# Six norms of a four-layer block: products on rows that are not yet normalised

## The chip, the cores and the metric

The kernel runs as one program on one core of a Trainium2 chip. The metric is the device time of one execution, in microseconds. TensorE (PE) multiplies, VectorE (DVE), ScalarE (ACT) and GpSimd (POOL) work on tiles of 128 partitions, and SyncE (SP) issues the transfers.

## What is computed

The input x is 256 tokens of 1024 channels. Four layers follow one another, two of a first kind and two of a second; each has a mixing part and a feed-forward part, and each part begins with an RMS norm:

```python
# first kind: norms before and after each part
h = rmsnorm(x, norm_mix_pre[l]);  z = h @ w_in[l]
x = x + rmsnorm(merged @ w_o[l], norm_mix_post[l])
h = rmsnorm(x, norm_ffn_pre[l]);  up = causal_dwconv(h @ w_up[l], ffn_conv_w[l])
x = x + rmsnorm((silu(gate) * val) @ w_down[l], norm_ffn_post[l])
# second kind: norms only before each part
xn = _rms(x, norm_mix_g);  z = xn @ w_in
x = x + merged @ w_out
xn = _rms(x, norm_ffn_g);  x = x + (silu(xn @ w_g) * (xn @ w_u)) @ w_down
# the norm
rmsnorm(x, g) = x * rsqrt(mean(x * x) + eps) * g
```

The factor rsqrt(...) is one number for each token, so that (x * g * factor) @ w is the same as ((x * g) @ w) * factor.

## The kernel before

**Layout.** x lies channel-major in X: eight row tiles of 128 channels by 256 tokens. All weights come as one stream of 582 pieces of 128 x 1024 (512 KB), each with eight blocks of 128 x 128. A ring of five buffers takes each piece from memory (F); ACT rounds it to H (high part), DVE subtracts it into L (low part), and PE uses both. DVE makes the low part of a piece at most four pieces ahead of PE, since the ring has five buffers. A product of one weight block with one row tile is three matmuls of 256 columns: high by high (HH), high by the row's low part (HL), low by high.

**Norms.** There are eight, numbered b = 0 to 7: b = 2 * layer for the mixing part, one more for the feed-forward part. Norms 1 to 4 (SUMMED) sit on the output of a post-norm of the first kind: there the last product of the layer before gives Z, the sum of squares of Z gives a first factor ("s1"), X becomes X + Z * factor, and only then comes the second factor ("s2") of the new X. Norms 0, 5, 6 and 7 are plain: one factor. In each norm PE adds the squares over partitions with a matrix of ones, ACT takes a root, DVE takes the reciprocal and makes a diagonal (line 1143), PE spreads it over the partitions (s1 or s2), and DVE multiplies the eight rows (line 1234 plain, line 1199 summed). ACT rounds each row to HH (line 1922), DVE (even rows, line 1248) and POOL (odd rows, line 2445) make HL. PE issues some idle matmuls (keep_busy) meanwhile, and then the first products of the next part.

**Order.** Nothing is scheduled at run time: every engine has its own program in a fixed order, written by functions that walk over the same list of groups. A group is one output tile of 128 columns (24 matmuls) or, where four are woven, four tiles in four PSUM banks (96 matmuls); a token group ("t", the values v, m_v) has 512-column products in two banks. PE takes the four banks in turn, and waits before a group until the bank's last reader (ACT or DVE) is done. `settle(n)` reads the banks of group n and stands in the programs beside group n + 1. In the mixing part of the first kind the groups are: the woven cf_b0, cf_a0, cf_b1, cf_a1, then cf_b2, cf_a2, cf_b3, cf_a3, then q0, q1, k0, k1, v, g_ret and so on. DVE also runs the 31 taps of a long convolution there (lines 1466 and 1470), four instructions beside each group. In the second kind they are: the woven i_q0, i_q1, gate8, i_k, then the token group m_v, then m_q0, m_q1, m_q2. In the feed-forward part: the woven fg0, fv0, fg1, fv1, then fg2, fv2.

**Swaps.** q and k are turned by a rotation; SP copies them with partitions exchanged (line 2626), and DVE waits for it (line 1302). SP issues weight pieces in front of the swap, and piece j of the stream waits until the low part of piece j - 5 is made:

```python
def asked(n):
    return G[n].pos // PB + 9
...
pieces_to(asked(group_of(l, name, 1) + 1))
swap(name, l, member(l, name, 1))
```

If p0 is the first piece of the woven group, q0 is piece p8, k0 is p10, and the swap of q waits for the issue of p18, and so for the low part of p13.

## Time and profile before

| | |
|---|---|
| median of 3 runs | 1834.47 us (1834.27 to 1837.68) |
| profiled execution, first to last instruction (span) | 1830.6 us |
| runs' median less that span (start and end of the program) | 3.9 us |
| PE busy | 1777.5 us, 97% of the span |
| DVE busy | 1360.9 us, 74% |
| ACT busy | 1073.6 us, 59% |
| granted TensorE clock | full in all 40 slices |

The profile was taken in one execution; no time of its own is given for that execution beside its span. A sum of parts is made against the span, and the 3.9 us around it are taken as unchanged. Times in a trace are counted from the first instruction. A row of the trace gives the start, the duration, and in brackets how long the engine was idle before it and what it waited for.

### The profile page before, as it was taken

The numbers are of one execution on the slowest core, as the hardware profiler recorded it, in microseconds if no ns is written. First come the engines' busy times: TensorE is split into PE (matmuls) and PEld (weight loads), VectorE is DVE, ScalarE is ACT, GpSimd is POOL, SyncE is SP. The second block draws the span as 40 slices with busy tenths as digits, with TensorE's granted clock in tenths as the row PEclk, the third lists the DMA queues.
The fourth block names the chain that finished last, engine by engine and source line by source line (L and its number), as shares of the span: only waits on it lengthen the run. The fifth ranks groups of instructions, "written<-read, shape, count | busy, mean of one in ns | idle before, by whom it ended". The sixth has DMA issues, their size and how long they took to land.

```text
span 1830.6 us, 36315 instructions
## 1 busy us (share of the span) xinstructions
PE 1777.5 (97%) x14784; PEld 1731.1 (95%) x14784; DVE 1360.9 (74%) x2385; ACT 1073.6 (59%) x1808; POOL 191.1 (10%) x200
## 2 busy tenths in 40 slices
PE   8999999999999999999999989999999998999998
PEld 8999999999999999999999879999999998899998
DVE  6898789867889779876768868655557697686553
ACT  5455666655455657654776576544458757755442
POOL 1002410001002410001201003000002100020000
PEclk9999999999999999999999999999999999999999
DMA  7545546564645536664645634556545564346563
GB/s 282 175 158 185 182 138 201 194 207 143 204 160 180 184 128 209 194 206 140 193 150 169 203 104 143 180 196 196 194 151 184 161 200 130 107 168 197 196 195 105
DMA packets 90341, 320.06 MB, mean 175 GB/s; under 512 B 10528, under 2 KB 12992, under 8 KB 90048
## 3 DMA queue, kind: packets, MB, share of 16 engines
q1 hardware_dynamic: 90176, 317.75, 53.7%
q8 instruction: 117, 1.92, 0.4%
q14 instruction: 48, 0.39, 0.1%
HBM read 310.60 MB, written 1.08 MB: 170 GB/s over the span
## 4 chain that ended last, share of the span: by engine, by line
PE 74%; DVE 15%; ACT 5%; issue 3%; POOL 1%; DMA 1%; SPq 0%; DVEq 0%; ACTq 0%; POOLq 0%
PE big L589 68%; PE small L589 4%; DVE L L1113 4%; DVE POOL L1470 4%; ACT H L1889 1%; PE small L588 1%; DVE POOL L1302 1%; DVE POOL L1668 1%; POOL POOL L2485 1%; ACT POOL L2311 1%; ACT POOL L2273 1%; ACT L1985 0%; POOL POOL L2464 0%; DVE FL L1280 0%; DVE POOL L1309 0%
## 5 line engine op out<-in xcount | busy, mean ns | idle before, releaser
L589 PE MATMUL big<-HH,H 128*128 128x256 f32 x3344 | 940.1, 281 | 5.3 <-ACT HH L1922 3.3
L589 PE MATMUL big<-HL,H 128*128 128x256 f32 x3344 | 925.2, 277 | 3.9 <-DVE HL L1248 3.8
L589 PE MATMUL big<-HH,L 128*128 128x256 f32 x3344 | 924.3, 276 | 0.0
L1113 DVE TENSOR_TENSOR L<-F,H 128x1024 fp32r<-128x1024 f32 x574 | 703.8, 1235 | 203.0 <-ACT H L1889 201.7
L1889 ACT ACTIVATE H<-F 128x1024 fp32r<-128x1024 f32 x582 | 610.7, 1055 | 205.7 <-PE big L589 202.8
L589 PEld LDWEIGHTS big<-HH,H 128*128 128x128 f32 x3344 | 628.2, 188 | 10.7 <-issue 5.5
L589 PEld LDWEIGHTS big<-HL,H 128*128 128x128 f32 x3344 | 628.4, 188 | 7.5 <-DVE HL L1248 5.7
L589 PEld LDWEIGHTS big<-HH,L 128*128 128x128 f32 x3344 | 627.9, 188 | 0.0
L589 PE MATMUL big<-FH,H 128*128 128x256 f32 x848 | 238.5, 281 | 0.0
L589 PE MATMUL big<-FH,L 128*128 128x256 f32 x848 | 234.4, 276 | 0.0
L589 PE MATMUL big<-FL,H 128*128 128x256 f32 x848 | 234.4, 276 | 0.0
L589 PEld LDWEIGHTS big<-FH,H 128*128 128x128 f32 x848 | 159.3, 188 | 1.4 <-issue 1.0
L589 PEld LDWEIGHTS big<-FL,H 128*128 128x128 f32 x848 | 159.3, 188 | 1.1 <-issue 1.0
L589 PEld LDWEIGHTS big<-FH,L 128*128 128x128 f32 x848 | 159.2, 188 | 0.0
L1470 DVE SCALAR_TENSOR_TENSOR POOL<-POOL,PR 128x256 f32<-128x256 f32 x240 | 104.1, 498 | 0.1
L589 PE MATMUL small<-POOL 128*128 128x128 f32 (+2 forms) x352 | 79.8, 347 | 11.5 <-DVE FL L1712 7.3
L589 PE MATMUL big<-ffn,H 128*128 128x256 f32 x512 | 88.4, 276 | 0.0
L589 PEld LDWEIGHTS big<-ffn,H 128*128 128x128 f32 x512 | 77.1, 188 | 0.0
L589 PEld LDWEIGHTS small<-POOL 128*128 128x128 f32 x352 | 53.0, 189 | 19.4 <-DVE FL L1712 9.2
L589 PE MATMUL big<-ffn,L 128*128 128x256 f32 x256 | 70.7, 276 | 0.0
L1371 DVE SCALAR_TENSOR_TENSOR POOL<-big,PR,POOL 128x255 f32<-128x255 f32 x88 | 42.2, 479 | 22.1 <-ACT POOL L2067 17.7
L2440 POOL TENSOR_TENSOR X<-X,POOL 128x256 f32<-128x256 f32 x16 | 15.1, 945 | 407.5 <-DVE POOL L1216 407.5
(237 smaller groups left out, 1797.4 us busy)
## 6 DMA issues: line engine op xcount, KB each, us to landing
F<-in_stream SPq DMA_DIRECT2D x582, 512.0 KB, 4.0
POOL<-POOL SPq DMA_DIRECT2D x32, 128.0 KB, 3.9
POOL<-head_rows SPq DMA_DIRECT2D x8, 256.0 KB, 5.1
X<-in_x SPq DMA_DIRECT2D x2, 512.0 KB, 4.8
POOL<-POOL SPq DMA_DIRECT2D x16, 64.0 KB, 3.0
out_x<-X SPq DMA_DIRECT2D x1, 1024.0 KB, 3.9
POOL<-in_decay SPq DMA_DIRECT2D x1, 768.0 KB, 11.1
POOL<-POOL SPq DMA_DIRECT2D x8, 96.0 KB, 5.7
```

Source lines behind the costliest of these rows:

```text
L588: return pe.e.matmul(out_, lhsT, rhs, start=start, stop=stop, skip_group_check=True)
L589: return pe.e.matmul(out_, lhsT, rhs, start=start, stop=stop)
L1113: v.tensor_tensor(L[:, j % NR, :], F[:, j % NF, :], H[:, j % NR, :].bitcast(F32), ALU.subtract).then_inc(s_lo, 1)
L1302: v.tensor_tensor(rows, rows, factor, ALU.mult).then_inc(rp_v[name].sem, rp_v[name].up(l, part))
L1371: v.scalar_tensor_tensor(out=dst[:, 1:T], in0=ps[:, 0:T - 1], scalar=par("ffn_w", l, 44 + row), in1=dst[:, 1:T], op0=ALU.mult, op1=ALU.add ...
L1470: r = v.scalar_tensor_tensor(out=acc, in0=glu[:, j, k:k + T], scalar=par("cf_w", l, k * 4 + j), in1=acc, op0=ALU.mult, op1=ALU.add)
L1668: r = v.tensor_tensor_reduce(out=p[:, e * nk:(e + 1) * nk], in0=bank[:, e * nk:(e + 1) * nk], in1=mask, scale=1.0, scalar=LOW, op0=ALU.add ...
L1889: a.activation(H[:, j % NR, :], F[:, j % NF, :], ACT.Copy).then_inc(s_hi, 1)
L2273: r = a.activation(p[:, e * nk:(e + 1) * nk], p[:, e * nk:(e + 1) * nk], ACT.Exp, bias=mx[:, e:e + 1], scale=root_of_queries("s_q", qt, pa ...
L2311: r = a.activation(p[:, e * nk:(e + 1) * nk], p[:, e * nk:(e + 1) * nk], ACT.Exp, bias=mx[:, e:e + 1], scale=root_of_queries("d_q", qt, h) ...
L2440: q.tensor_tensor(X[:, n, :], X[:, n, :], tile(Z + n), ALU.add).then_inc(bnd_g.sem, bnd_g.up(b, "x", n))
L2485: q.tensor_tensor(tile(dst), tile(x), tile(y), ALU.add).then_inc(lc_g.sem, lc_g.up(l, event))
```

## The change

For six norms (RAW: 0, 2, 4, 5, 6, 7) the first groups are computed from rows x * g that don't carry the token factor. RAW gives how many groups: five after norms 0 and 2, two after 4 and 6, one after 5 and 7. ACT rounds x * g (high_raw), DVE makes its low part (low_raw), into memory that is free at that time (ROUND, ffn). PE begins with these rows, and forms the sums and the spreading matmuls between the products of the woven group (beside_row); at a summed norm only the second factor is put off, the first is still needed for X. ACT copies the spread factor to a tile S in SBUF. DVE then multiplies each raw result by S from PSUM to a tile RAWT (scaled_out), and the former readers read RAWT; the token group m_v gets the factor as a scale of ACT's copy. The normalised rows are still made (normal_rows, high_rows), for the groups after the raw ones: beside the raw groups, two rows at a time. The order of the woven group's 96 matmuls changes: for each row four high-by-high, four high-by-low, four low-by-high. At the start SP issues the gains of norm 0 and the first weight piece before x. The idle matmuls of the six norms go.

```diff
+RAW = {0: 5, 2: 5, 4: 2, 5: 1, 6: 2, 7: 1}
...
+            def raw_blocks(g):
+                b, n = g.raw, len(g.members)
+                banks_ = [bank_for(m)[:, 0:T] for m in g.members]
+                for k in range(KT):
+                    if k == 3:
+                        yield
+                    places = []
+                    for i in range(n):
+                        j, o = divmod(g.pos + k * n + i, PB)
+                        places.append((j, H[:, j % NR, o * P:(o + 1) * P], L[:, j % NR, o * P:(o + 1) * P]))
+                    m = g.members[0]
+                    xh, xl = x_of(m, k)
+                    wait_x(m, k, False)
+                    for ps, (j, hi, lo) in zip(banks_, places):
+                        pe.wait_ge(s_hi, j + 1)
+                        mm(ps, hi, xh, start=(k == 0), stop=False)
+                    wait_x(m, k, True)
+                    for ps, (j, hi, lo) in zip(banks_, places):
+                        mm(ps, hi, xl, start=False, stop=False)
+                    for i, (ps, (j, hi, lo)) in enumerate(zip(banks_, places)):
+                        pe.wait_ge(s_lo, j + 1)
+                        r = mm(ps, lo, xh, start=False, stop=(k == KT - 1))
+                        if k == KT - 1 or (k * n + i + g.pos) % PB == PB - 1:
+                            r.then_inc(s_mm, 1)
+                    beside_row(b, k)
+            def beside_row(b, k):
+                if b in SUMMED:
+                    if k == 6:
+                        pe.wait_ge(bnd_v.sem, bnd_v.at(b, "dg2"))
+                        mm(use(3, b, "s2")[:, 0:T], ones, tile(DG + 1)).then_inc(s_fill[3], 1)
+                    return
+                if k == (6 if b == 0 else 0):
+                    if b == 0:
+                        bank = use(0, b, "yy")
+                        pe.wait_ge(s_ones, 16)
+                        pe.wait_ge(bnd_v.sem, bnd_v.at(b, "add", 0, 7))
+                        wide_sums(bank, (0, 1), tile(YSQ), True, True).then_inc(s_fill[0], 1)
+                    else:
+                        sums_of(b, 7, False, True)
+                if k == (7 if b == 0 else 2):
+                    pe.wait_ge(bnd_v.sem, bnd_v.at(b, "dg"))
+                    mm(use(2, b, "s1")[:, 0:T], ones, tile(DG)).then_inc(s_fill[2], 1)
+            def raw_norm(b):
+                if b not in SUMMED:
+                    return
+                yy, zx = use(0, b, "yy"), use(1, b, "zx")
+                pe.wait_ge(bnd_v.sem, bnd_v.at(b, "add", last_added(b)))
+                wide_sums(yy, (0, 1), squares_at(0), True, False)
+                pe.wait_ge(bnd_a.sem, bnd_a.at(b, "sq", 7))
+                wide_sums(yy, (0, 1), squares_at(7), False, True).then_inc(s_fill[0], 1)
+                wide_sums(zx, (0, 2), squares_at(0, 1), True, False)
+                wide_sums(zx, (1, 3), squares_at(0, 2), False, False)
+                pe.wait_ge(bnd_v.sem, bnd_v.at(b, "dg"))
+                mm(use(2, b, "s1")[:, 0:T], ones, tile(DG)).then_inc(s_fill[2], 1)
+                pe.wait_ge(bnd_a.sem, bnd_a.at(b, "zz", 7))
+                wide_sums(zx, (0, 2), squares_at(7, 1), False, False)
+                pe.wait_ge(bnd_v.sem, bnd_v.at(b, "xz", 7))
+                wide_sums(zx, (1, 3), squares_at(7, 2), False, True).then_inc(s_fill[1], 1)
...
+            def low_raw(b, k):
+                gain, l = gain_of(b)
+                dve.wait_ge(rh_a.sem, rh_a.at(b, k))
+                v.scalar_tensor_tensor(out=raw_low(b, k), in0=X[:, k, :], scalar=par(gain, l, k),
+                                       in1=raw_high(b, k).bitcast(F32), op0=ALU.mult, op1=ALU.subtract).then_inc(
+                    rl_v.sem, rl_v.up(b, k))
...
+            def raw_norm(b):
+                first = begun_pieces(first_of(b))
...
+                if b in SUMMED:
+                    product_of_sums(b, 7)
+                was_read(b, "yy")
+                v.reciprocal(col(4, 2), col(2, 2)).then_inc(bnd_v.sem, bnd_v.up(b, "r"))
+                dve.wait_ge(bnd_v.sem, bnd_v.at(b, "r"))
+                diagonals(col(4, 2), tile(DG), bnd_v, b, "dg")
+                if b in SUMMED:
+                    raw_rows(b)
+                    return
+                if b:
+                    dve.wait_ge(s_evd, (last_of(b // 2, "out") if b % 2 else last_of(b // 2 - 1, "down")).dve)
+                    low_raw(b, 7)
+                    low_parts(first + AHEAD + 1)
+                if b % 2:
+                    for pair in range(4):
+                        normal_rows(b, pair)
+                        if pair == 2:
+                            low_parts(first + AHEAD + 2)
...
+            def raw_rows(b):
+                u = kept(b)
+                scaled(b, 0)
+                added(b, 0)
+                for n in range(KT):
+                    if n % 2 == 0:
+                        for i in (n + 1, n + 2):
+                            if i < KT:
+                                scaled(b, i)
+                    if n % 2:
+                        dve.wait_ge(bnd_g.sem, bnd_g.at(b, "x", n))
+                    else:
+                        dve.wait_ge(bnd_v.sem, bnd_v.at(b, "x", n))
+                    low_raw(b, n)
+                    if n % 2 == 0 and n + 2 < KT:
+                        added(b, n + 2)
...
+            def normal_rows(b, pair):
+                layer, e = use_of(b)
+                gain, l = gain_of(b)
+                was_read(b, "s2" if b in SUMMED else "s1")
+                dve.wait_ge(s_par, 16)
+                for n in (2 * pair, 2 * pair + 1):
+                    v.scalar_tensor_tensor(out=normal(b, n), in0=X[:, n, :], scalar=par(gain, l, n), in1=S,
+                                           op0=ALU.mult, op1=ALU.mult).then_inc(bnd_v.sem, bnd_v.up(b, "full", n))
+                low_x(b, 2 * pair)
+            def scaled_out(m):
+                b, i = m.raw
+                was_read(b, "s2" if b in SUMMED else "s1")
+                if i >= 4:
+                    before = [x for g in G if g.raw == b for x in g.members][i - 4]
+                    dve.wait_ge(s_eva, before.act)
+                    dve.wait_ge(s_evd, before.dve)
+                dve.wait_ge(s_mm, m.done)
+                v.tensor_tensor(landed(m), big[m.banks[0]][:, 0:T], S, ALU.mult).then_inc(
+                    raw_v.sem, raw_v.up(b, i))
...
             def settle(n, low=0):
-                for m in G[n].members:
-                    if low:
+                for i, m in enumerate(G[n].members):
+                    if m.raw and m.kind != "t":
+                        scaled_out(m)
+                    if low and (i % 2 == 0 or not m.raw):
                         low_parts(low)
...
+                pairs = pairs_in(n)
                 for j in first:
+                    if len(pairs) > 1:
+                        normal_rows(g.raw, pairs.pop(0))
                     low_parts(j + AHEAD)
                 if not made_after and not tapped and not full_banks(n - 1):
                     settle(n - 1)
+                for pair in pairs:
+                    normal_rows(g.raw, pair)
...
+            def high_raw(b, k):
+                gain, l = gain_of(b)
+                a.activation(raw_high(b, k), X[:, k, :], ACT.Copy, scale=par(gain, l, k)).then_inc(
+                    rh_a.sem, rh_a.up(b, k))
...
+                bank, read = is_filled(b, "yy")
+                root(col(2, 2), sums_in(bank), D).then_inc(read, 1)
+                if b in SUMMED:
+                    square_of_sums(b, 7)
+                    high_parts(first + AHEAD + 1)
+                    for n in range(KT):
+                        if n % 2:
+                            act.wait_ge(bnd_g.sem, bnd_g.at(b, "x", n))
+                        else:
+                            act.wait_ge(bnd_v.sem, bnd_v.at(b, "x", n))
+                        high_raw(b, n)
+                        if n in (3, 5):
+                            high_parts(first + AHEAD + n // 2 + 1)
+                    act.wait_ge(bnd_v.sem, bnd_v.at(b, "u"))
+                    root(col(6, 2), kept(b), D).then_inc(bnd_a.sem, bnd_a.up(b, "v"))
+                tables(layer, e)
+                if b not in SUMMED and b:
+                    high_parts(first + AHEAD + 2)
+                bank, read = is_filled(b, "s2" if b in SUMMED else "s1")
+                a.activation(S, bank[:, 0:T], ACT.Copy).then_inc(read, 1)
+                if b % 2:
+                    for pair in range(4):
+                        high_rows(b, pair)
+                        if pair % 2 == 0:
+                            high_parts(first + AHEAD + 3 + pair // 2)
+            def high_rows(b, pair):
+                layer, e = use_of(b)
+                for n in (2 * pair, 2 * pair + 1):
+                    act.wait_ge(bnd_v.sem, bnd_v.at(b, "full", n))
+                    a.activation(HH[:, n, :], normal(b, n), ACT.Copy).then_inc(hh.sem, hh.up(layer, e, n))
...
+                pairs = pairs_in(n)
                 for j in first:
+                    if len(pairs) > 1:
+                        high_rows(g.raw, pairs.pop(0))
                     high_parts(j + 1 + AHEAD)
+                for pair in pairs:
+                    high_rows(g.raw, pair)
...
+            c = pcol["mix_pre0"]
+            q.dma_start(PR[:, c:c + KT], params[:, c:c + KT]).then_inc(s_gain, 16)
+            pieces(0, 1)
             q.dma_start(X[:, 0:4, :], xT[:, 0:4, :]).then_inc(s_x, 16)
+            pieces(1, 3)
             q.dma_start(X[:, 4:8, :], xT[:, 4:8, :]).then_inc(s_x2, 16)
             q.dma_start(CO[:, 0:256], consts[:, 0:256]).then_inc(s_ones, 16)
-            pieces(0, 2)
-            q.dma_start(PR[:, :], params).then_inc(s_par, 16)
-            pieces(2, NF)
+            pieces(3, 4)
+            q.dma_start(PR[:, c + KT:], params[:, c + KT:]).then_inc(s_par, 16)
+            pieces(4, NF)
             q.dma_start(CO[:, 256:], consts[:, 256:]).then_inc(s_const, 16)
             q.dma_start(tile(DEC, 6), decay).then_inc(s_dec, 16)
             done[0] = NF```

`order` of DVE in layer 0, from the bank reads of the woven group to the low part of piece p13 (line numbers of the kernel before; L1113 is a weight piece's low part, L1257 the product of cf_a with its factor, L1466 and L1470 are taps of the long convolution). Before:

```order
L1113 TENSOR_TENSOR L<-F,H 128x1024 x2
L1257 TENSOR_TENSOR POOL<-big,POOL 128x256
L1113 TENSOR_TENSOR L<-F,H 128x1024 x2
L1257 TENSOR_TENSOR POOL<-big,POOL 128x256
L1466 TENSOR_SCALAR POOL<-POOL,PR 128x256 x4
L1113 TENSOR_TENSOR L<-F,H 128x1024
L1470 SCALAR_TENSOR_TENSOR POOL<-POOL,PR 128x256 x4
L1113 TENSOR_TENSOR L<-F,H 128x1024
```

The same place now, from the last part of it (L1254 is the low part of a piece, L1410 scaled_out, L1528 the product of cf_a, L1397 the normalised rows, L1519 their low part, L1743 and L1747 the taps):

```order
L1254 TENSOR_TENSOR L<-F,H 128x1024
L1410 TENSOR_TENSOR RAWT<-big,POOL 128x256
L1397 SCALAR_TENSOR_TENSOR POOL<-X,PR,POOL 128x256 x2
L1519 TENSOR_TENSOR HL<-POOL,HH 128x256
L1254 TENSOR_TENSOR L<-F,H 128x1024
L1410 TENSOR_TENSOR RAWT<-big,POOL 128x256
L1528 TENSOR_TENSOR POOL<-RAWT,POOL 128x256
L1743 TENSOR_SCALAR POOL<-POOL,PR 128x256 x4
L1254 TENSOR_TENSOR L<-F,H 128x1024
L1747 SCALAR_TENSOR_TENSOR POOL<-POOL,PR 128x256 x4
L1254 TENSOR_TENSOR L<-F,H 128x1024
```

The rows' products and their low parts stood ahead of the woven group's reads and now stand behind them, and eight reads (L1410) have come in; the taps and the low part of p13 stand behind all of these.

ACT beside the token group m_v of layer 2, before (L1955 reads i_q, L1977 gate8, L1991 to L1994 i_k, L1889 rounds a weight piece, L2189 to L2193 are parts of the mLSTM's factors, L1959 reads m_v and frees its two banks):

```order
L1994 ACTIVATE POOL<-big 4x256
L1889 ACTIVATE H<-F 128x1024 x6
L2189 ACTIVATE POOL<-POOL,PR 4x256
L2191 ACT_TABLE_LOAD
L2191 ACTIVATE POOL<-POOL 4x256
L2193 ACT_TABLE_LOAD
L2193 ACTIVATE POOL<-POOL 4x256
L1959 ACTIVATE POOL<-big 128x512
```

The same place now (L2355 reads i_k's last rows, L2249 rounds the normalised rows, L2173 a weight piece, L2553 to L2557 are the mLSTM's, L2320 reads m_v):

```order
L2355 ACTIVATE POOL<-RAWT 4x256
L2249 ACTIVATE HH<-POOL 128x256 x2
L2173 ACTIVATE H<-F 128x1024 x2
L2249 ACTIVATE HH<-POOL 128x256 x2
L2173 ACTIVATE H<-F 128x1024
L2249 ACTIVATE HH<-POOL 128x256 x4
L2173 ACTIVATE H<-F 128x1024 x2
L2553 ACTIVATE POOL<-POOL,PR 4x256
L2555 ACT_TABLE_LOAD
L2555 ACTIVATE POOL<-POOL 4x256
L2557 ACT_TABLE_LOAD
L2557 ACTIVATE POOL<-POOL 4x256
```

Eight roundings of rows have come between the weight pieces and the mLSTM's instructions; the read of m_v stands behind them as before.

## Rows read from the trace of the kernel before

**Rows 1.** The page: busy time of engines, and DVE in 40 slices

```profile
PE 1777.5 (97%) x14784; PEld 1731.1 (95%) x14784; DVE 1360.9 (74%) x2385; ACT 1073.6 (59%) x1808; POOL 191.1 (10%) x200
...
DVE  6898789867889779876768868655557697686553
```

**Rows 2.** Timeline around norm 6, plain: start, duration, instruction, idle before

```profile
1341.10 0.28 PE L589 MATMUL big<-ffn,L 128*128 128x256 f32 x1
...
1344.66 1.05 PE L589 MATMUL small<-CO 128*128 128x128 f32 x8
...
1346.38 0.39 PE L589 MATMUL big<-HL,H 128*128 128x256 f32 x1
```

**Rows 3.** Timeline around norm 2, summed

```profile
430.12 0.28 PE L589 MATMUL big<-ffn,L 128*128 128x256 f32 x1
```

**Rows 4.** The chain that ended last, from norm 2 on

```profile
439.15 56.83 PE big L589 x449
```

**Rows 5.** PE's timeline at the start

```profile
12.45 1.91 PE L589 MATMUL small<-CO 128*128 128x128 f32 x8
...
14.35 0.28 PE L589 MATMUL big<-HL,H 128*128 128x256 f32 x1
```

**Rows 6.** DVE's timeline in norm 2 and behind it

```profile
437.96 0.47 DVE L1199 SCALAR_TENSOR_TENSOR POOL<-X,PR,small 128x256 f32<-128x256 f32 x1
438.35 0.41 DVE L1216 TENSOR_TENSOR POOL<-POOL,small 128x256 f32<-128x256 f32 x1
438.68 0.42 DVE L1248 TENSOR_TENSOR HL<-POOL,HH 128x256 fp32r<-128x256 f32 x1
...
451.25 2.36 DVE L1113 TENSOR_TENSOR L<-F,H 128x1024 fp32r<-128x1024 f32 x2 [1.21 <-ACT H L1889]
...
461.52 1.38 DVE L1466 TENSOR_SCALAR POOL<-POOL,PR 128x256 f32<-128x256 f32 x4
462.80 1.22 DVE L1113 TENSOR_TENSOR L<-F,H 128x1024 fp32r<-128x1024 f32 x1
463.94 1.68 DVE L1470 SCALAR_TENSOR_TENSOR POOL<-POOL,PR 128x256 f32<-128x256 f32 x4
465.52 1.23 DVE L1113 TENSOR_TENSOR L<-F,H 128x1024 fp32r<-128x1024 f32 x1
```

**Rows 7.** The chain that ended last, in layer 0

```profile
41.46 1.15 DVE L L1113
...
42.62 0.33 SPq L2601
...
44.90 3.92 DMA POOL<-POOL
```

**Rows 8.** DVE's timeline later in layer 1

```profile
478.67 1.22 DVE L1113 TENSOR_TENSOR L<-F,H 128x1024 fp32r<-128x1024 f32 x1 [0.95 <-ACT H L1889]
...
488.50 0.42 DVE L1332 TENSOR_TENSOR POOL<-big,POOL 128x256 f32<-128x256 f32 x1
...
491.56 0.42 DVE L1332 TENSOR_TENSOR POOL<-big,POOL 128x256 f32<-128x256 f32 x1
```

**Rows 9.** PE's longest waits in the retention of layers 0 and 1

```profile
77.14 0.92 PE L589 MATMUL small<-POOL 128*128 128x256 f32 x4 [1.90 <-DVE POOL L1430]
...
500.18 0.92 PE L589 MATMUL small<-POOL 128*128 128x256 f32 x4 [0.79 <-DVE POOL L1430]
```

**Rows 10.** ACT's timeline in layer 2, behind the woven group

```profile
872.18 0.72 ACT L1955 ACTIVATE POOL<-big 128x256 f32<-128x256 f32 x2 [2.14 <-PE big L589]
...
875.06 4.87 ACT L1889 ACTIVATE H<-F 128x1024 fp32r<-128x1024 f32 x5
...
883.11 1.28 ACT L2191 ACT_TABLE_LOAD   x1
...
886.57 0.60 ACT L1959 ACTIVATE POOL<-big 128x512 f32<-128x512 f32 x1
```

**Rows 11.** DVE and POOL side by side in layer 0

```profile
139.90 1.99 POOL L2472 TENSOR_TENSOR POOL<-POOL 128x256 f32<-128x256 f32 x1 [1.88 <-DVE POOL L1447]
...
141.21 2.15 DVE L1470 SCALAR_TENSOR_TENSOR POOL<-POOL,PR 128x256 f32<-128x256 f32 x4
```

278 lines of the change are left out of this document (227 added, 51 removed).

## The prediction

> **What bounds the kernel now.** I read the page first. PE is busy 97% of the span and DVE 74%, but DVE's slices reach 9 in the first part of the program [rows 1]. So time can be won only where PE stands still, and where DVE is nearly full any work added to DVE can come back as a wait of PE. Then I read PE's timeline at the norms. At norm 6, a plain one, the last product of the part before starts at 1341.10 and products flow again from 1346.38: 5.2 us [rows 2] (5.3 at norms 5 and 7). At norm 2, a summed one, 430.12 [rows 3] stands against the 439.15 at which the chain of waits goes into PE's long stretch [rows 4]: 9.0 us, and as much at norm 4. In the first layer products begin at 14.35 [rows 5]. These gaps are what the change works on. Last I looked for the places where PE waits behind DVE in the same layers: in the retention of layer 0 it waits 1.90 us at 77.14, in layer 1 0.79 us at 500.18 [rows 9]. The chain of waits tells how the first of these comes about: a low part made by DVE at 41.46, then SP at 42.62, then the swap's transfer at 44.90 [rows 7]. From there on DVE works without a pause until PE's wait.
>
> **Prices.** From DVE's timeline behind norm 2 [rows 6], start to start: the product of one row or bank with a factor tile 0.33 (438.35 to 438.68), one with three inputs 0.39 (437.96 to 438.35), the low part of a piece 1.14 (462.80 to 463.94), four taps 1.28 of one kind and 1.58 of the other. A matmul of 256 columns takes about 0.1135, a group of one tile (24) 2.72, four woven tiles (96) 10.9. ACT needs 0.97 for a piece's high part (4.87 for 5) and 0.36 for a bank [rows 10].
>
> **What it removes: the gaps.** In a plain norm the products need only x and the gain, and the sums and the factor's spreading are set between rows. After the last product come 10.9 of products, 0.9 of sums and spreading and some 0.3 for row 7, which is ready last: at norm 6 the woven group ends near 1353.5, where it ended at 1346.4 + 10.9 = 1357.3. That is 3.8 earlier; at norms 5 and 7, 3.3, since there the sums wait about 0.5 more for the sixth row behind a short group. In a summed norm the first factor still has to come; after it DVE must bring eight rows by 0.33 + 0.39 and four sums of 0.33, 7.1 in all. The group ends near 446.5 for 439.15 + 10.8 = 449.9: 3.4 earlier, the same in norm 4. At the start products can begin when rows and the first piece are there, near 7.3. But PE's matmuls take about twice their time until 14 (the same eight idle ones 1.91 at 12.45, 1.05 at 1344.66 [rows 2, 5]), so 7.3 to 14 is worth 3.35 of products and the group ends near 14 + 7.55 + 0.7 = 22.3 for 14.2 + 10.9 and waits = 25.5: 3.2 earlier. Heads alone: 3.2 + 3.4 + 3.4 + 3.3 + 3.8 + 3.3 = 20.4 us faster.
>
> **What it adds.** For each raw output tile one product with the factor on DVE (8, 8, 6, 4, 6, 4 of them), two-input low parts become three-input ones, and in norms 0, 2, 4 and 6 the normalised rows, their high and low parts move from ahead of the woven group to behind it. The reads of the banks, and then everything queued on DVE, stand behind this.
>
> **Layers 0 and 1 (norms 0 and 2): a loss.** Between the first read of a woven bank and the low part of p13 DVE now has 8 reads (0.34 each), 4 products with the factor (1.36), 9 low parts (10.3), 8 normalised rows (3.1), 4 low rows (1.36), two sets of taps (1.3 and 1.6): 21.8 us. Waits between them (ACT's rounding of a row before its low part, the factor for the pairs) I put at 2.5 to 3: the handover to ACT and back is 0.36 and two steps of 0.1, once in each of four pairs, and the reads start before PE has filled all banks. GpSimd's four operations may cost 0.5 to 1 more: four taps took 2.15 beside one of GpSimd's [rows 11], and 1.68 at 463.94 [rows 6]. So p13 is made at 22.3 + 21.8 + 2.75 + 0.75 = 47.6 in layer 0 (47.1 to 48.1), where it was made at 41.46 + 1.15 = 42.6 [rows 7]: 5.0 later though the head is 3.2 earlier. The swap of q stands behind the issue of p18, and this waits for p13. Its 4 us of transfer follow, then DVE's chain, which has no idle in it to lose the delay in: its own rounds take 3.06 us (488.50 to 491.56 [rows 8]) against PE's 2.72. So PE's wait at 77.14 grows by the whole 5.0. In layer 1 the same sum from 446.2 gives 471.5 (471.0 to 472.0), where the low part was done at 465.52 + 1.23 = 466.75 [rows 6]: 4.75 later. There DVE has a pause of 0.95 at 478.67 [rows 8] that takes so much of it, and smaller ones I count as 0.3: 3.5 remain (2.8 to 4.1). The wait at 500.18 grows by that. Below, the bound is no loss at all, if DVE's added work fits into its pauses (one of 1.21 stands at 451.25 [rows 6]); above, the full 4.75 and the same again in the swap of k, 6.
>
> The Trainium skill ("Advanced Engine Details and Errata", section VectorE Performance Modes) says that the second SBUF port of VectorE is shared with GpSimd, and that instructions on it "will interfere/block eachother". The row of 2.15 agrees. Were each of the eight moved low parts and normalised rows held up as long as GpSimd runs, by that page the loss in each layer would be some 2 us more; the sum above does not use this.
>
> **Layer 2 and layer 3 (norms 4 and 6).** The token group m_v needs banks 0 and 1, and m_q2 needs bank 0 back from ACT's read of m_v. Before, ACT read m_v at 886.57, behind a table load of 1.28 [rows 10], and m_q2 began 16.35 after the woven group's end. Now eight roundings of rows (8 by 0.36, with handovers) stand ahead of it: 6 reads, 5 or 6 high parts, 8 roundings and the mLSTM's part end 19.5 (norm 4) and 20.4 (norm 6) after the group, and 0.7 is added for waits on DVE. Norm 4: 869.5 + 20.2 = 889.7 for 872.9 + 16.35 = 889.2, 0.5 slower. Norm 6: 1353.5 + 21.1 = 1374.6 for 1357.3 + 16.35 = 1373.7, 0.9 slower. Bounds: nothing added by ACT (3 faster), all of DVE's waits passed on (2 slower).
>
> **Norms 5 and 7.** No swap and no token group behind them. DVE's normalised rows stand ahead of its first bank read, which falls about 1.2 behind the group's end, and the next group waits for bank 0: 1.6 with the read. 3.3 less 1.6 is 1.7 faster each (0.8 to 2.5).
>
> **The sum.** 5.0 + 3.5 + 0.5 - 1.7 + 0.9 - 1.7 = 6.5 us slower. The span of 1830.6 becomes 1837.1; with the 3.9 outside it the time is 1841.0. The runs' median 1834.5 is that of this execution (1830.6 + 3.9), so it needs no correction. I say 1841.
>
> **The rivals.** *The gains stay* (chance 0.15). If p13 is made at or before 42.6 in layer 0, nothing is later than before and the 3 us heads are kept in most norms: 20.4 less about 1.6 in each of norms 5 and 7 and up to 6 in the others, 12 to 17 us faster, 1817 to 1822. For it: DVE had pauses between the reads and p13, as the 1.21 at 451.25 [rows 6]. Against it: 21.8 us of work from 22.3 can't end before 44.1, even without a wait, and by then the swap is already 1.5 late. *DVE's delay is partly absorbed* (0.12): q and k come late, but g_ret's groups let DVE catch up; half the loss in the first two layers goes and norms 4 and 6 keep 1 each, 1828 to 1830.5. *They cancel* (0.25): the loss in each of layers 0 and 1 is 2 less, or norms 4 and 6 gain what they should, 1831 to 1838. *Much worse* (0.08): the swaps of k and the taps fall behind too, or GpSimd's port costs each layer 2 more, and two layers lose 10 each: above 1847. The forecast itself has 0.40 between 1838 and 1847.
>
> **How the numbers follow.** 0.2% is 3.7 us, about what a measurement of this kernel can tell from none. Slower 0.40 + 0.08 = 0.48, within 0.25, faster 0.27. The range leaves out the worst case (0.08) and most of the case in which gains stay (0.13): 1828 to 1847. The forecast's own range is 1838 to 1844, from 2.8 to 5.5 lost in each of the first two layers and the bounds of the rest by halves.
>
> **What would show it.** The first products at 7.3; no gap above 1 us at norms 5, 6 and 7, one of about 5.5 at norms 2 and 4; the low part of p13 near 47.6 and the wait behind it at the retention grown to 5 to 7 us in layer 0 and 3 to 4 in layer 1; about 2 us of wait for ACT before m_q2; about 1 us before the first group behind norms 5 and 7. The forecast is wrong if p13 comes before 44, if the retention waits do not grow while p13 is late (then DVE's chain has slack that I don't see), or if the groups behind q start late without a wait for DVE.

## The result, and the profile after

The changed kernel takes 1858.09 us (median of 4 runs, 1857.24 to 1860.25) against 1834.37: ratio 1.0133, 95% interval 1.0116 to 1.015. It is slower, as forecast, but by 23.7 us where 6.5 were. The profiled execution (1858.5 us from first to last instruction) is 27.9 us longer than the profiled one of before.

The page of the changed kernel, busy time and DVE's slices (answers to [rows 1]):

```profile
PE 1783.9 (96%) x14676; PEld 1733.1 (93%) x14676; DVE 1394.1 (75%) x2464; ACT 1095.6 (59%) x1858; POOL 205.9 (11%) x204
...
DVE  7998789867999779876867867755558687687553
```

PE is busy 6 us longer with 108 fewer matmul records. The reason stands in the granted clock. A table by stretches of the changed kernel; the last three numbers of a row are TensorE's clock, the DMA share and GB/s:

```profile
34.00:38.00 4.00, 3.14 (x24) 2.63 (x22) 3.44 (x7) 2.36 (x6) 1.80 (x1) 1.00 0.51 171
38.00:42.00 4.00, 1.82 (x8) 1.15 (x7) 3.13 (x7) 2.37 (x6) 1.97 (x2) 0.86 0.56 199
42.00:46.00 4.00, 3.29 (x14) 3.00 (x15) 3.90 (x8) 1.94 (x3) 1.53 (x1) 0.50 0.39 132
```

Behind a stretch in which PE was busy for 1.82 of 4 us, the clock is at 0.50, the lower of its two levels (1.2 of 2.4 GHz). There are seven such falls, of 3.4 or 6.8 us each, 34 us in all (the profile of before had none ahead of its end). The Trainium skill ("TensorE: Matmul & The Clock Gate", Part 1) says that "the default state is throttled, and activity releases the throttle"; this trace agrees in that the clock was 0.50 behind the less busy stretch. The page of the profile does not show the falls:

```profile
PEclk9999999999999999999999999999999999999999
```

This row is the same in both kernels. A 9 stands for 90% or more, and a fall of 3.4 us takes only 4% off a slice of 46 us. Over the whole span the granted clock is 0.990 in this profile and 1.000 in that of before.

To see where the time goes I took, for the same weight piece, the start of ACT's rounding in both traces, and subtracted. Lateness in us added at each norm and what follows it until the next (pieces 76, 100, 200, 250, 330, 400, 513, 581; worked out from the timelines), and the time at half clock in that part:

```
kernel       norm 0     1     2     3     4     5     6     7   sum
changed        5.1    1.6   5.7   1.6   4.9   4.1   3.6   1.3  27.9
 half clock    6.8    3.4   6.8   3.4   3.4   6.8   3.4   0
hold           8.2    1.7   4.7   0     3.5   3.4   3.8   3.1  28.4
 half clock    6.8    3.4   0     0     0     0     0     0
hold2          7.2    0     5.3   0     3.6   1.7   3.9   1.4  23.2
 half clock    6.8    0     0     0     3.4   0     3.4   0
pace57         4.5    1.6   6.9   0     3.4  -1.4   3.7  -1.7  17.1
 half clock    6.8    3.4   6.8   0     3.4   0     3.4   0
taps_before   -2.8    0     0.6  -0.1   1.7   0.2   0.1   0    -0.4
 half clock    0      0     3.4   0     3.4   0     0     0
taps_after     3.7    0     3.9   0     6.6   2.9   5.3   3.9  26.3
 half clock    6.8    0     6.8   0     6.8   6.8   3.4   6.8
rows32         4.5    1.7   5.7   1.7   2.6  -1.4   6.4  -1.7  19.5
 half clock    6.8    3.4   6.8   3.4   0     0    10.2   0
order2         8.9    0.1   7.2   0     5.0  -1.5   5.5  -1.7  23.5
 half clock   10.2    0     6.8   0     3.4   0     3.4   0
lowlate        5.1    0     9.1   1.6   2.4  -1.4   4.5  -1.6  19.8
 half clock    6.8    0    10.2   3.4   3.4   0     6.8   0
lowlate_c      5.4    0     5.4   0     2.4  -1.4   4.4  -1.6  14.6
 half clock   10.2    0     6.8   0     3.4   0     6.8   0
both           5.5    0     5.0  -0.1   1.2  -1.4   2.2  -1.8  10.6
 half clock    6.8    0     6.8   0     3.4   3.4   3.4   0
best57        -0.9    1.7   3.1   0     0.1  -1.9  -0.2  -1.7   0.1
 half clock    0      3.4   3.4   0     0     0     3.4   0
best57c       -1.7    0     1.0  -0.1   0    -1.8  -0.3  -1.7  -4.5
 half clock    0      0     0     0     0     0     0     0
```

One profile scatters: norms 0 and 2 of best57 and best57c are code of before, and read -1.7 to 3.1 (with a fall in best57's norm 2). Differences under some 1.5 us at one norm are read only where they repeat. Norms 1 and 3 have the same code in both kernels: they lose 1.6 or 1.7 where a fall of 3.4 us lies in them, and nothing where none does.

PE's timeline, layer 0, in the first q group and at the retention (answers to [rows 9]):

```profile
37.71 0.39 PE L655 MATMUL big<-HH,H 128*128 128x256 f32 x1 [0.63 <-ACT HH L2249]
...
39.89 0.38 PE L655 MATMUL big<-HL,H 128*128 128x256 f32 x1 [1.09 <-POOL HL L2811]
...
41.40 0.58 PE L655 MATMUL big<-HH,H 128*128 128x256 f32 x1 [1.01 <-ACT HH L2249]
...
43.58 0.58 PE L655 MATMUL big<-HL,H 128*128 128x256 f32 x1 [0.71 <-POOL HL L2811]
...
82.39 0.48 PE L655 MATMUL small<-POOL 128*128 128x256 f32 x1 [0.76 <-DVE POOL L1707]
```

The low part of p13, DVE's timeline (answers to [rows 7]): it ends at 48.95.

```profile
47.74 1.21 DVE L1254 TENSOR_TENSOR L<-F,H 128x1024 fp32r<-128x1024 f32 x1
```

Norm 5, ACT, DVE and PE around the last raw rows:

```profile
1172.99 0.41 DVE L1673 TENSOR_TENSOR X<-X,big 128x256 f32<-128x256 f32 x1
...
1173.50 0.42 ACT L2448 ACTIVATE POOL<-X 128x256 f32<-128x256 f32 x1 [1.68 <-DVE X L1673]
1173.82 0.49 ACT L2186 ACTIVATE ffn<-X,PR 128x256 fp32r<-128x256 f32 x1
1174.22 1.05 ACT L2173 ACTIVATE H<-F 128x1024 fp32r<-128x1024 f32 x1
...
1175.30 1.22 DVE L1254 TENSOR_TENSOR L<-F,H 128x1024 fp32r<-128x1024 f32 x1
1176.44 0.41 DVE L1673 TENSOR_TENSOR X<-X,big 128x256 f32<-128x256 f32 x1
...
1178.67 1.22 PE L654 MATMUL small<-CO,POOL 128*128 128x128 f32 x4 [3.35 <-DVE POOL L1691]
...
1195.46 0.38 PE L655 MATMUL big<-HH,H 128*128 128x256 f32 x1 [1.55 <-DVE RAWT L1410]
```

From one X row to the next is 3.45 us (1172.99 to 1176.44; the rows ahead of it came 3.39 and 3.45 apart, and in norm 7 it is the same): DVE adds the row, ACT squares it, rounds it and then rounds the next weight piece, DVE makes that piece's low part and only then adds the next row. PE's group takes 2.72. PE pays at the end, 3.35 us before the sums. In the kernel before the same rows came 3.05 apart and PE waited 0.58 us there (at 1157.68); the raw row's rounding on ACT adds about 0.4 to each turn.

Norm 4, behind the woven group (answers to [rows 10]):

```profile
892.47 0.81 ACT L2249 ACTIVATE HH<-POOL 128x256 fp32r<-128x256 f32 x2 [1.49 <-DVE POOL L1397]
893.18 1.04 ACT L2173 ACTIVATE H<-F 128x1024 fp32r<-128x1024 f32 x1
895.39 0.81 ACT L2249 ACTIVATE HH<-POOL 128x256 fp32r<-128x256 f32 x2 [1.16 <-DVE POOL L1397]
...
903.65 0.66 ACT L2320 ACTIVATE POOL<-big,SCR 128x512 f32<-128x512 f32 x1
...
904.93 0.39 PE L655 MATMUL big<-HH,H 128*128 128x256 f32 x1 [2.02 <-ACT POOL L2321]
```

ACT stands idle 3.6 us among the roundings (1.49, 1.16, and further down 0.49 and 0.46), and reads m_v 3.2 us later than it would by the lateness of 13.9 that it came with.

### The profile page after: what moved, and what is told of

Read it like the earlier page. It is cut to its first block, busy times and chain, and to the rows that moved or that the text cites. A ratio compares the mean times of both kernels' runs of the same rounds, so it can differ in the third digit from the quotient of the medians.

```text
span 1858.5 us, 36279 instructions
## 1 busy us (share of the span) xinstructions
PE 1783.9 (96%) x14676; PEld 1733.1 (93%) x14676; DVE 1394.1 (75%) x2464; ACT 1095.6 (59%) x1858; POOL 205.9 (11%) x204
## 2 busy tenths in 40 slices
DVE  7998789867999779876867867755558687687553
## 4 chain that ended last, share of the span: by engine, by line
PE 69%; DVE 17%; ACT 8%; issue 4%; POOL 2%; DMA 0%; SPq 0%; DVEq 0%; ACTq 0%; POOLq 0%
PE big L655 63%; DVE L L1254 5%; PE small L655 4%; DVE POOL L1747 3%; ACT H L2173 2%; PE small L654 1%; DVE POOL L1397 1%; DVE POOL L1945 1%; DVE POOL L1573 1%; POOL POOL L2871 1%; ACT POOL L2637 1%; ACT POOL L2675 1%; ACT HH L2249 0%; DVE HL L1519 0%; ACT L2346 0%
## 5 line engine op out<-in xcount | busy, mean ns | idle before, releaser
L655 PE MATMUL big<-HH,H 128*128 128x256 f32 x3088 | 874.9, 283 | 13.6 <-ACT POOL L2321 4.0
L655 PE MATMUL big<-HL,H 128*128 128x256 f32 x3088 | 860.3, 279 | 6.3 <-POOL HL L2811 4.3
L655 PE MATMUL big<-HH,L 128*128 128x256 f32 x3088 | 858.6, 278 | 0.0
L1254 DVE TENSOR_TENSOR L<-F,H 128x1024 fp32r<-128x1024 f32 x578 | 708.0, 1232 | 185.3 <-ACT H L2173 182.5
L2173 ACT ACTIVATE H<-F 128x1024 fp32r<-128x1024 f32 x582 | 611.3, 1054 | 202.8 <-PE big L655 191.8
L655 PEld LDWEIGHTS big<-HH,H 128*128 128x128 f32 x3088 | 585.2, 190 | 19.7 <-ACT POOL L2321 4.4
L655 PEld LDWEIGHTS big<-HL,H 128*128 128x128 f32 x3088 | 585.5, 190 | 10.9 <-POOL HL L2811 5.7
L655 PEld LDWEIGHTS big<-HH,L 128*128 128x128 f32 x3088 | 585.0, 189 | 0.0
L655 PE MATMUL big<-FH,H 128*128 128x256 f32 x848 | 238.5, 281 | 0.0
L655 PE MATMUL big<-FH,L 128*128 128x256 f32 x848 | 234.4, 276 | 0.0
L655 PE MATMUL big<-FL,H 128*128 128x256 f32 x848 | 234.3, 276 | 0.0
L655 PEld LDWEIGHTS big<-FH,H 128*128 128x128 f32 x848 | 159.3, 188 | 1.4 <-issue 1.0
L655 PEld LDWEIGHTS big<-FL,H 128*128 128x128 f32 x848 | 159.3, 188 | 1.1 <-issue 1.0
L655 PEld LDWEIGHTS big<-FH,L 128*128 128x128 f32 x848 | 159.2, 188 | 0.0
L655 PE MATMUL big<-ffn,H 128*128 128x256 f32 x640 | 107.9, 280 | 0.0
L1747 DVE SCALAR_TENSOR_TENSOR POOL<-POOL,PR 128x256 f32<-128x256 f32 x240 | 103.7, 492 | 0.1
L655 PEld LDWEIGHTS big<-ffn,H 128*128 128x128 f32 x640 | 94.6, 191 | 0.2
L655 PE MATMUL small<-POOL 128*128 128x128 f32 (+2 forms) x352 | 79.8, 347 | 13.6 <-DVE FL L1989 7.4
L655 PE MATMUL big<-ffn,L 128*128 128x256 f32 x320 | 81.0, 278 | 0.0
L2811 POOL TENSOR_TENSOR HL<-POOL,HH 128x256 fp32r<-128x256 f32 x32 | 39.8, 1243 | 326.8 <-ACT HH L2249 315.0
L655 PEld LDWEIGHTS small<-POOL 128*128 128x128 f32 x352 | 53.0, 189 | 21.5 <-DVE FL L1989 9.2
L655 PE MATMUL big<-ROUND,H 128*128 128x256 f32 x384 | 60.0, 286 | 11.2 <-ACT ROUND L2186 8.4
```

What stands on the lines that cost most here:

```text
L655: return pe.e.matmul(out_, lhsT, rhs, start=start, stop=stop)
L1254: v.tensor_tensor(L[:, j % NR, :], F[:, j % NF, :], H[:, j % NR, :].bitcast(F32), ALU.subtract).then_inc(s_lo, 1)
L1747: r = v.scalar_tensor_tensor(out=acc, in0=glu[:, j, k:k + T], scalar=par("cf_w", l, k * 4 + j), in1=acc, op0=ALU.mult, op1=ALU.add)
L2173: a.activation(H[:, j % NR, :], F[:, j % NF, :], ACT.Copy).then_inc(s_hi, 1)
L2811: q.tensor_tensor(HL[:, n, :], normal(b, n), HH[:, n, :].bitcast(F32), ALU.subtract).then_inc(hl_g.sem, hl_g.up(layer, e, n))
```

## The experiments

**One kind of site at a time.** `RAW` cut to {0: 5, 2: 5}, to {4: 2, 6: 2} and to {5: 1, 7: 1}.

> The changed kernel with the raw products in norms 0 and 2 alone (the two mixing parts of the first kind). Theory A: the loss is made site by site, each site of its own new waits of PE plus the half clock that these waits bring on. By the high parts of the pieces, before against changed, norms 0 and 2 lose 5.3 and 5.5 us, and the unchanged norms 1 and 3 lose 1.4 and 1.5 by 3.4 us each at half the clock: 11 us slower than before if the half clock at norms 1 and 3 does not come, 14 if it does. Rival B: the sites act on each other (the phase of everything behind a late norm 0), so that the three parts do not add up to the whole 24 to 28 us.

> The changed kernel with the raw products in norms 4 and 6 alone (the mixing parts of the second kind). Theory A: 5.3 + 3.7 = 9 us slower than before, of which 2 x 1.7 are two stretches of 3.4 us at half the clock and the rest the 2 us waits of PE for ACT's read of m_v before m_q2 and a later wait in the mLSTM; the granted clock stays full in layers 0 and 1. Rival B: other than 9 by more than 3 us.

> The changed kernel with the raw products in norms 5 and 7 alone (the feed-forward parts of the second kind). Theory A: 3.7 + 1.2 = 4.9 us slower than before: PE stands 3.35 us before the sums and 1.55 before the second group in both, and one stretch of 6.8 us at half the clock falls into norm 5. If the half clock falls in neither, 1.5 slower; in both, 8.

1847.94, 1847.96 and 1847.71 us: ratios 1.0066 (1.0042 to 1.009), 1.0073 (1.0048 to 1.0097), 1.0075 (1.005 to 1.0101). They stand against a kernel before of 1834.9 beside them, so the three lose 13.0, 13.1 and 12.8 us, 38.9 together, where the whole change loses 23.7. They don't add up, and rival B is right for two reasons. Without norm 0 in `RAW` the new order of the first loads still delays the old norm 0, by 3.5 us at the first piece, so two of the three carry a loss that is not the change's. And all three have the falls at norms 1 and 3 that the whole change has too, so these 3.3 us are counted three times. By the norms themselves: only02 loses 4.4 and 5.8, only46 6.6 and 5.3 (10.2 us at half clock), only57 3.0 and 3.4 (3.4 us in each).

**Keeping PE busy in its waits.**

```diff
+                    if late and k in (4, 6):        # late: the first q group
+                        keep_busy(3, 2 * k - 4)
...
+                    if b in (5, 7):
+                        keep_busy(3, 24)
                     pe.wait_ge(bnd_v.sem, bnd_v.at(b, "add", last_added(b)))
```

> The changed kernel with idle matmuls of 128 columns issued ahead of PE's new waits, so that PE stays busy there: 20 in each of the first q groups of layers 0 and 1 (rows 4 to 7), 24 before the sums of norms 5 and 7, 14 before the second m_q group of layers 2 and 3. No wait is taken away. Theory A (the half clock costs its 34 us / 2 = 17 us on top of the waits): with the clock full again at these places the time falls by 8 to 13 us from 1858, to 1845 to 1850. Rival B (at half the clock PE only uses up time that it would wait anyway, since DVE and ACT set the pace there): the clock is full and the time falls by less than 3 us. Rival C: the clock does not follow PE's idle time at these places, and the half stretches stay.

1862.89 us, 1.0151 (1.013 to 1.0172). The filler was twice too long (an idle matmul is two records of 0.11 us), so PE was late by it: norms 0 and 7 lose 3 and 2 more. Theory A's 1845 to 1850 is missed, and the run shows only that the clock follows: 0.994 to 0.997 for 0.990 to 0.992.

> As hold, with the idle matmuls at half the number, since each is two passes of PE and took 0.11 us a pass: 13 in each first q group (3.0 us for waits of 3.4), 12 ahead of the sums of norms 5 and 7 (2.8 for 3.35), 7 ahead of the second m_q group. No wait is taken away and little time is added. Theory A (the half clock is a cost of its own at these places): norms 0 and 2 keep their 5.3 and 5.5, as the wait at the retention takes the place of the half clock there, norm 5 falls from 3.7 to about 1.3, norms 4 and 6 from 5.3 and 3.7 to 3.5 and 2: 1849 to 1854. Rival B: the half clock only fills time in which PE waits for DVE or ACT everywhere, so the time stays at 1856 to 1860 though the clock is full.

1856.4 us, 1.0101 (1.0077 to 1.0125), clock 0.995 to 0.996. The time lies in rival B's range, while the places differ. The first q groups are at full clock, and norm 5 falls from 4.1 to 1.7, as theory A said. But norm 2 loses 5.3 at full clock for 5.7, so at half clock PE there used up for the most part a wait that it had anyway (at the retention of layer 1 it waits 2.82 us now, 1.11 in the changed kernel); and in norm 0 the wait came back at the retention, with the fall behind it:

```profile
81.62 0.79 PE L655 MATMUL small<-POOL 128*128 128x256 f32 x1 [2.63 <-DVE POOL L1716]
```

```profile
42.00:46.00 4.00, 3.57 (x31) 3.38 (x31) 3.90 (x10) 1.34 (x2) 0.79 (x1) 1.00 0.42 133
82.00:86.00 4.00, 4.00 (x18) 3.82 (x18) 3.18 (x6) 1.44 (x2) 0.00 (x0) 0.50 0.58 176
```

The first fence is hold2's timeline, the second its stretches.

**The chain at norms 5 and 7.**

```diff
+                if g.layer > 1 and g.members[0].label == "out" and not made_after:
+                    low_parts(pieces_in(g)[0][-1] + AHEAD)      # DVE, ahead of the row's low part
                 staged.step()
...
+                    high_parts(first[-1] + 1 + AHEAD)           # ACT, ahead of settle(n - 1)
```

> The changed kernel with another order in the out products of layers 2 and 3 alone: ACT rounds the next weight piece before the square and the rounding of the row, and DVE makes the low part of the piece before the low part of the raw row. Theory (in the changed kernel these form one chain: X row on DVE, square, rounded row and piece on ACT, low part of the piece on DVE, next X row, 3.45 us a group against PE's 2.72, which adds up to PE's wait of 3.35 before the sums): the wait before the sums falls below 1 us in norms 5 and 7, and the pieces' lateness there from +3.9 and +1.3 to about 0 and -1.5: 4 to 6 us less than the changed kernel, 1852 to 1854. Rival: the wait comes from the raw rows' added work on DVE and ACT itself, whatever its order, and stays above 2.5 us.

1850.67 us, 1.0066 (1.0044 to 1.0088), 7.4 below the changed kernel, more than the 4 to 6 expected. Norms 5 and 7 now gain 1.4 and 1.7. Not all of that is the chain: in norm 5 the fall of 6.8 us is gone as well. Against hold2, which has no fall there either, the order is worth 3.1 us in each of the two (1.7 to -1.4 and 1.4 to -1.7). PE's timeline of pace57 has no wait before the sums, and the other wait as before:

```profile
1172.97 0.71 PE L654 MATMUL small<-CO,POOL 128*128 128x128 f32 x4
...
1187.49 0.39 PE L655 MATMUL big<-HH,H 128*128 128x256 f32 x1 [1.56 <-DVE RAWT L1410]
```

The X rows come 2.2 to 2.6 us apart. No work was taken away, so the chain is shown, not only argued.

**DVE's total work in layers 0 and 1.** Ten taps on 32 of 256 columns, in both kernels:

```diff
+                            w = 32 if k > 19 else T
-                            r = v.scalar_tensor_tensor(out=acc, in0=glu[:, j, k:k + T], ...
+                            r = v.scalar_tensor_tensor(out=acc[:, 0:w], in0=glu[:, j, k:k + w], ...
```

> The kernel before, with the taps 29 to 20 of the long convolution done on 32 of their 256 columns, so most of that work is left out: about 10 us less work for DVE in layer 0 and as much in layer 1. It is the partner of the next one. Both theories: PE's waits at the retention (1.90 and 0.79 us) go, so 2 to 3 us faster than before, 1831 to 1833.

> The changed kernel with the same taps left out in the same way. Theory (norms 0 and 2 lose because DVE is full between the woven group and the retention): the waits behind the swap go with DVE's work, and by the pieces norms 0 and 2 lose at most 1 us each, where they lost 5.3 and 5.5; set against its partner, 8 to 11 us of the 24 are gone, so 1845 to 1849. Rival (the loss is in the first q group, where PE waits 3.7 us for normalised rows, before any of these taps matter much): by the pieces norm 0 still loses 4 or more, norm 2 too, and the time is 1855 to 1857.

1831.13 us (0.9969, 0.9955 to 0.9983) and 1859.5 (1.0142, 1.0086 to 1.0198). The first is as expected, the second above both ranges. Norm 0 still loses 3.7 against a partner that gains 2.8: 6.5 apart, where it was 5.1 with all taps. PE's waits in the first q group are unchanged, and neither kernel waits at the retention any more. So PE's loss in the first q group, its waits and the half clock together, is enough for all of norm 0's, and DVE's work is not needed for it. It does not follow that DVE has slack with all its taps: in hold2, where PE was only 3.8 us late behind the first q group (6.4 in the changed kernel), DVE still held the retention until 81.62, 4.5 us later than in the kernel before. Norm 0 has two limits of nearly one height, and taking DVE's away leaves the other. At norm 2 the two are 3.3 apart for 5.7, but taps_before has a fall of 3.4 us in that part, so it is not shown how much of the 2.4 is DVE's. The second run's time is above the rival's range because of what comes later: norms 4 to 7 have 24 us at half clock (13.6 in the changed kernel) and lose 18.7 for 13.9.

**The pairs of normalised rows.** rows32 makes them on 32 of 256 columns in norms 2, 4 and 6; order2 moves ACT's and DVE's instructions; both stand on pace57.

```diff
+                    w = 32 if b in (2, 4, 6) else T          # rows32
-                    v.scalar_tensor_tensor(out=normal(b, n), in0=X[:, n, :], ...
+                    v.scalar_tensor_tensor(out=normal(b, n)[:, 0:w], in0=X[:, n, 0:w], ...
...
+                if g.layer < 2 and pairs and pairs[0] > 1:   # order2, ahead of ACT's high_parts
+                    high_rows(g.raw, pairs.pop(0))
```

> As pace57, but in norms 2, 4 and 6 the eight normalised rows are made by DVE on 32 of their 256 columns, so seven eighths of that work is left out (8 instructions shorter by some 0.27 us each, 2.2 us a norm); norm 0 is as in pace57 and is the control. Theory (behind the woven group, DVE, ACT and GpSimd hand the normalised rows to each other, about 3.5 us a pair against PE's 2.72 a group, and in layers 2 and 3 ACT stands idle 3.6 us waiting for them; shorter rows on DVE pass on): by the pieces norm 2 loses 2 us less than its 5.5, norms 4 and 6 lose 1.5 to 2 less than 3.3 each, and the time is 1844 to 1846. Rival (ACT's own work sets the end there, DVE's rows do not): norms 4 and 6 stay within 0.5 of 3.3.

> As pace57, with two changes of order. Layers 0 and 1: for the last two pairs of normalised rows ACT rounds the rows ahead of the next weight piece (1.04 us). Layers 2 and 3: DVE makes the first two pairs of rows ahead of the low parts of two pieces, ACT rounds them there too. Theory (each step of a pair waits for an engine that is doing something else, not for a lack of total work): PE's waits in the first q group fall from 3.4 to below 2, ACT's idle time among the roundings in layers 2 and 3 from 3.6 to about 2.5, and the time by 2 to 5 us against pace57, to 1846 to 1849. Rival (total work of DVE counts): the pairs come no sooner and the time stays within 1 us of 1850.7.

rows32: 1850.18 us (1.0072, 1.0059 to 1.0085). Norm 4 loses 2.6 for 3.4, but pace57 had a fall of 3.4 us there and rows32 none, so little is shown by it; norm 2's waits stay (3.2 us for 3.4 in the first q group). The 1844 to 1846 expected are missed. Its DVE timeline shows why: the time that the shorter rows give back is spent waiting for ACT, which stands behind a weight piece:

```profile
461.44 0.56 DVE L1398 SCALAR_TENSOR_TENSOR POOL<-X,PR,POOL 128x32 f32<-128x32 f32 x2
...
461.94 1.04 ACT L2177 ACTIVATE H<-F 128x1024 fp32r<-128x1024 f32 x1
...
463.32 0.43 DVE L1521 TENSOR_TENSOR HL<-POOL,HH 128x256 fp32r<-128x256 f32 x1 [1.32 <-ACT HH L2253]
```

order2: 1856.94 us (1.0111, 1.0096 to 1.0125), a miss: PE's waits in the first q group fell from 3.4 to 2.7, but the weight pieces came later for it and the wait at the retention grew to 3.56 (at 84.45), and norms 4 and 6 lost more.

> As pace57, with one change of order on DVE in norms 0, 2, 4 and 6: the low part of a normalised row, for which DVE waits until ACT has rounded the row, stands behind the low part of the next weight piece and no longer ahead of it. No work is added or taken away. Theory (each pair of rows goes round DVE, ACT and DVE again in fixed queues, 3.4 us a pair whatever DVE's own work): the pair comes to 2.7 to 3.0 us, PE's waits in the first q group fall from 3.4 to below 1.5, and norms 0 and 2 lose 2 us less each unless the wait at the retention takes it up; in norm 4 ACT's idle time among the roundings falls from 3.6 to about 2: 1844 to 1848 for 1850.7. Rival (total work of DVE): the waits in the first q group shrink but the retention's grow by the same, and the time stays within 1 us of 1850.7.

```diff
+                    while behind:                # DVE, behind the piece's low part
+                        low_x(*behind.pop(0))
```

> As lowlate, with more idle matmuls in the unchanged norms 1 and 3 (7 for 4 ahead of the second factor's spreading, 6 for 4 ahead of the first product). Theory: the half clock at norms 1 and 3 (3.4 us each, 1.5 to 1.7 us of loss by the pieces) goes in all executions, 2 to 3 us faster than lowlate, the granted clock up by 0.002. Rival: it was in part of the executions only, and the medians differ by less than 1.

> As lowlate_c, and as in rows32 the eight normalised rows of norms 2, 4 and 6 are made on 32 of 256 columns, so that DVE has both less work and no wait for ACT there; norm 0 is as in lowlate_c and is the control. Theory (two limits of nearly the same height, each of which hides the other): a pair of rows comes every 2.8 to 3.0 us in layer 1, PE's waits in its first q group fall from 4.5 (lowlate_c) to below 2.5, and by the pieces norm 2 loses 1.5 us less than in lowlate_c. Rival (a third limit, such as ACT's own work): the pairs stay at 3.4 and the waits at 4.

lowlate 1852.51 us (1.0081, 1.0049 to 1.0113), no faster than pace57, and 1844 to 1848 expected: PE's waits in the first q groups grew from 3.4 to 4.5 and 4.9, now for DVE's low parts and ACT's roundings. lowlate_c 1847.4 (1.0061, 1.0042 to 1.0081): 5.1 below lowlate, 2 to 3 expected. By the table norm 3, which got idle matmuls, gives 1.6 of it; norm 2 gives 3.7, where the two have the same code and lowlate's profile has a fall of 3.4 us more, so that part is not shown to be the idle matmuls' work. both, 1842.77 (1.0033, 1.002 to 1.0045): PE's waits in layer 1's first q group are 3.9 (4.5 in lowlate_c), the first and last pair 9.2 us apart for 10.2, and norm 2 loses 5.0 for 5.4. Most of the loss stays though DVE has less work and doesn't wait for the rounded rows. So its cause in norms 0 and 2 is settled to a place, not to an engine: the rows pass DVE, ACT and GpSimd, whose queues hold weight pieces in between, slower than PE's groups. In norm 4 DVE's work counts: 2.4 us lost in lowlate_c, 1.2 in both, with the same 3.4 us of half clock. PE's wait is another one there than in the changed kernel, though: it is for DVE's low part of a row (3.52 us at 897.78 in lowlate_c, 2.30 at 896.18 in both), no longer for ACT's read of m_v. Norm 6 shows the same two waits (3.31 and 2.06).

**The parts that gain, alone.**

```diff
-RAW = {0: 5, 2: 5, 4: 2, 5: 1, 6: 2, 7: 1}
+RAW = {5: 1, 7: 1}
...
-                keep_busy(3, 4)          # best57c, norms 1 to 4
+                keep_busy(3, 7)
```

> Raw products in norms 5 and 7 alone, with the order of pace57 and the order of the first loads of the kernel before. Theory (pace57 gains 1.7 in each of norms 5 and 7, and all else of the change loses): 3.4 us faster than the kernel before, ratio 0.998, norms 0 to 4 and 6 as before. Rival (the gain shows only behind the other norms): no difference.

> As best57, with more idle matmuls in norms 1 to 4: 7 for 4 ahead of the second factor's spreading, 6 for 4 ahead of the first product. Theory (half clock stretches of 3.4 us come in some executions of every kernel at these gaps, by the granted clock of 0.995 to 1.000 in the runs of the kernel before, and cost 1.7 us each): the granted clock is nearer to 1 and the median 1 to 3 us below best57. Rival (the number does not matter, the remaining waits are enough for a fall): the same clock, and up to 1 us slower by the idle matmuls themselves.

best57: 1832.03 us, 0.9976 (0.9966 to 0.9986), faster than the kernel before (1836.51 beside it). No run has the order of pace57 without raw rows; but as the kernel before waits only 0.58 us at that place, the order by itself has little to give there. best57c: 1829.93, 0.9966 (0.9954 to 0.9979), the fastest; its clock is 0.998 to 0.999 in all runs, where the kernel before had 0.996 to 0.999 beside it. The intervals of the two overlap, so that best57c is faster than best57 is likely, not shown.

## Why the prediction was wrong

**Direction and bound: right.** PE loses where it waits on DVE and ACT, and the heads do not carry it. The profiles are 27.9 us apart for 6.5 forecast. Of the 21.4 between, 6.4 lie in norms 5 and 7, 5.5 in norms 4 and 6, 1.8 in norm 2, 0.1 in norm 0, and 7.6 in the clock.

**Norm 0: the size right, the mechanism half.** 5.0 forecast, 5.1 measured. p13's low part came at 48.95, forecast 47.6 (before 42.6 [rows 7]); from DVE's first read of a bank it took 25.4 us, forecast 25.3. The instruction behind the retention's wait starts 5.25 later (82.39 for 77.14). But "PE's wait at 77.14 grows by the whole 5.0" is wrong: it shrank to 0.76, one of the signs that I had named for a wrong forecast. PE had lost the time already in the first q group (0.63 + 1.09 + 1.01 + 0.71 = 3.4 us, which the prediction did not price) and then ran 6.8 us at half clock. The reason that I had given with the sign, slack in DVE's chain, does not hold either: in hold2 the wait is 2.63. Two losses lie side by side, and that their end fits the forecast so well is in part luck. Also the head gave less than the 3.2 forecast: DVE's first read of a bank is at 23.52, not 22.3, since ACT's copy of the factor (23.10) stands behind a table load of 1.28.

**Norm 2: 3.5 forecast, 5.3 without the clock (hold2).** The same unpriced waits of the first q group, 3.4 us; the wait at the retention is 1.11 for 0.79, and 2.82 in hold2. The sum for this layer also starts from 446.2, where the head had given 446.5; that is 0.3 of the difference.

**Norms 5 and 7: the step that failed with the wrong sign.** The prediction let the sums "wait about 0.5 more for the sixth row"; the wait is 3.35 in both. It had priced instructions and not the ring through two queues, so the head's 3.3 us were lost again before the sums. With the ring cut (pace57) the gain is 1.4 and 1.7, forecast 1.7; the term of 1.6 for bank 0 measured 1.55.

**Norms 4 and 6: 0.5 and 0.9 forecast, 3.3 and 3.6 measured** (norm 4 ahead of the fall in it). "0.7 is added for waits on DVE" was 3.6 us of idle time of ACT in norm 4 and 3.0 in norm 6. And ACT has no slack behind m_v: it stays 17.2 late from there on, so PE's slack before m_q2 saved nothing.

**The clock: no term had it.** Without it the waits make 5.1 + 5.3 + 3.3 + 1.7 + 3.6 + 1.3 = 20.3 of the 27.9 us; the rest, 1.6 in each of norms 1 and 3, 0.4 in norm 2, some 1.6 in norm 4 and 2.4 in norm 5, is 7.6. Norm 6's fall cost nothing that can be read: the norm loses 3.9 in hold2 with the fall, and 3.8 in hold without it but with 3.1 us of idle matmuls behind the wait (1397.37 to 1400.51), so PE is not the bound there. In norm 0 no run has full clock throughout. By hold2, which is 4.5 late at the retention and has its fall only behind it, what the fall took in the first q group came back as a shorter wait there. The 0.4 of norm 2 is less than one profile can tell. The runs of before had falls too (clocks of 0.995 to 1.000), its profile none; so the medians are 23.7 apart and the profiles 27.9.

**The rivals.** "Much worse" had the size, above 1847, by a mechanism that it did not name: neither the swaps of k nor a port. The GpSimd term is small: in norm 0 of the changed kernel DVE's low parts of rows at 34.37 and 41.38 take 0.42, since GpSimd's run next to them hardly at all. In lowlate, where DVE's stands beside GpSimd's, three of four in layer 0 take 0.95 (the one at 38.57, say). The 2 us more in each layer did not come: from the first read to p13's low part it took 25.4 us for the 25.3 forecast without them.

## What to carry to other kernels

When work moves from ahead of a group to behind it, don't add up durations: write down for each moved item which queue it passes, and what stands in that queue in front of it. A ring through two in-order queues has a period of its own (3.45 us here against PE's 2.72), it shows only at its end as one long wait, and reordering two instructions can cut it. Count the engine behind the wait as well: slack of PE is worth nothing if ACT comes out of it full. And try a change site by site; here two of six sites gained, once the ring was cut.
